# The experts of a mixture-of-experts stage: blocks of 64 rows in plain fp32 on halves of the array, in place of blocks of 128 rows in split products

## The chip, the cores and the metric

The kernel runs on one core of a Trainium2 chip. The metric is the device time of one execution in microseconds. The core has five engines with a queue each: TensorE (PE: matmuls and transposes into the eight PSUM banks), VectorE (DVE), ScalarE (ACT), GpSimd (POOL) and SyncE (SP, which here only issues DMAs). They meet through semaphores; each engine's instructions start in the order written.

## The reference

Two networks run one after the other on 512 tokens of width 1024, everything in fp32. The first has a recurrent group, a banded attention, a cross attention on a memory of 256 rows, and a mixture of 32 experts; the second has two layers with attention and a feed-forward part. Only the experts matter here:

```python
# ht: (512, 1024); every token goes to 2 of 32 experts, with weights combine_w
def expert_block(args):                  # a block of rows of one expert
    xb, e = args
    g = xb @ w_gate[e]                   # (rows, 1024) @ (1024, 512)
    u = xb @ w_up[e]                     # (rows, 1024) @ (1024, 512)
    return (jax.nn.silu(g) * u) @ w_down[e]   # (rows, 512) @ (512, 1024)
ys = lax.map(expert_block, (xs, block_expert))
contrib = ys[dest] * w_sorted[:, None]
y = zeros((512, 1024)).at[tok_sorted].add(contrib)     # then x + y, and two norms
```

With the reference's inputs the 1024 (token, expert) pairs fall on the 32 experts as 35 42 69 32 24 45 40 43 21 7 30 35 45 21 28 23 33 48 31 61 61 41 28 25 20 21 15 22 24 11 27 16. The kernel finds this on the chip; any routing has to work.

## The kernel before

**Products.** Nearly all products are split: a matrix is written as a high part in fp32r and a low part, the rest, and high x high, high x low and low x high are summed in PSUM, three matmuls for one. ScalarE writes the high parts, VectorE subtracts to get the low ones. For the experts' weights these are `weights_high` (L722, the activation at L726) and `weights_low` (L556, L558), in six units an expert: 0 and 1 gate, 2 and 3 up, 4 and 5 down.

**Ahead of the experts.** The cross attention ends with its output product (TensorE L1953), to which the router's products are added (L2085). `moe_tensor` (L448) turns the normed rows (`rows(HR, n)`, L458); ScalarE evacuates them scaled (L734) and stores each row twice to `rows_scratch` in DRAM (L736), 1 MB per tile of 128 tokens. VectorE works out the routing in some forty small operations (L564 to L640). The rank of each pair within its expert comes from triangular matmuls (L468, L472), and the list of rows of every expert from eight matmuls on one-hot ranks (L475), which leave `idx` (L611). Then TensorE turns the rows of X (L458 again), which ScalarE keeps as `AUX` (L747).

**The loop.** A block holds up to 128 rows of one expert. GpSimd gathers its rows from DRAM (`gather`, L406); TensorE turns them (`turn_x`, L484), ScalarE and VectorE split them (L754, L647). `unit` (L487, matmuls L494) takes the six units in order: 48 matmuls of 128x512 for gate and up, 24 for down. In between come silu (L767), the product with up (L662), its transposes (L522) and its split (L783, L670). The down product of a block runs behind the gate and up products of the next. Its 128x1024 result is evacuated (`lay_y`, L759, L760) and stored to `expert_rows` in DRAM at its rows' places by an indirect DMA (`store`, L409). The three weight matrices of an expert, 2 MB each, are loaded by SyncE (L358, L362) into `ring[0]`, `ring[1]` and `ring[2]`, one buffer each, as soon as both parts of the previous one are split. Blocks beyond the 32nd, for experts with more than 128 rows, use lists from a table in DRAM (`slot_tokens`, L417, L421); there are none with these inputs.

**Behind the loop.** SyncE loads the stored rows back (L389); VectorE adds both of a token's rows, weighted, to X (L699, L700) and multiplies by the norm's weights (L702); ScalarE sums rows and squares (L808, L810, L811); two roots (L814, L815) and a scaling (L715, L818) follow; TensorE turns the result back (L545), and the first layer's products begin (L1031).

The next lines are the heart of the loop on TensorE.

```python
for k in range(n_k):
    for q, (i, w) in enumerate(((0, e_high(u)), (0, e_low(u)), (1, e_high(u)))):
        for j in range(n_j):
            mm = pe.matmul(acc[j][:, :], xs[i][:, (u % 2) * n_k + k, :], w[:, n_j * k + j, :], ...)
```

The attention further behind has plain fp32 matmuls on parts of the array: `pe_pairs` (L1717) has two heads in the two halves of the rows for the scores (L1729) and in the two halves of the columns for the values (L1744), each followed by transposes (L1760). L1068 is a plain fp32 sum over partitions with the whole array.

Of the kernel before, what the change touches and what calls it, by code (L numbers as in the profile page):

```python
# [37 lines left out]
SLOTS = 2 * T  # L38
OVER = (SLOTS - 1) // (P + 1)
MAXB = EXPERTS + OVER  # L40
MINB = EXPERTS
ABSENT = 2 * SLOTS
# [36 lines left out]
CONSTS = [("ident", P), ("ones", P), ("lower", P), ("pair", P), ("perm", P), ("perm32", P), ("desc", EPG), ("count", P), ("slot", 2 * TT)]  # L79
# [34 lines left out]
def build(nc, A, out):  # L114
    with ExitStack() as ctx:
# [71 lines left out]
        s_bias = sem("bias_ready")  # L187
# [57 lines left out]
        slots = sb("slots", [P, 2, TT], U32)  # L245
        ids = sb("ids", [P, 2, TT], U32)
        absent = sb("absent", [P, OVER], U32)
# [4 lines left out]
        LAG = 3  # L252
        idx_more = sb("idx_more", [P, 2 + LAG], U32)
        rows_dram = nc.dram_tensor("rows_scratch", (SLOTS, D), F32).ap()
        slot_dram = nc.dram_tensor("slot_tokens", ((LAG + 1 + OVER + 2 * TT) * P, 1), U32).ap()
        y_dram = nc.dram_tensor("expert_rows", (SLOTS, D), F32).ap()
        HT = S[:, 0:8, :].rearrange("p (t a) n -> p t (a n)", t=TT)
        XROW = AUX[:, :, :].rearrange("p (t a) n -> p t (a n)", t=TT)
        FROW = X[:, 0:2, :].rearrange("p a n -> p (a n)")
        Y = [[S[:, 4 * t + 2 * w:4 * t + 2 * w + 2, :].rearrange("p a n -> p (a n)") for w in range(2)] for t in range(TT)]  # L260
        JUNK = [S[:, 16:18, :].rearrange("p a n -> p (a n)"), S[:, 18:20, :].rearrange("p a n -> p (a n)"), QKVG[:, 0:2, :].rearrange("p a n -> p (a n)")]
        HR = MKV[:, 0:DC, :]
# [20 lines left out]
        hot_ids = S[:, 20, 0:2 * TT * EXPERTS].rearrange("p (w t n) -> p w t n", w=2, t=TT)  # L283
# [4 lines left out]
        XB = S[:, 8:10, :].rearrange("p a n -> p (a n)")  # L288
        XBT = [SP[:, i:i + 2, :].rearrange("p a (c s) -> p (a c) s", s=P) for i in (10, 12)]
        SG, PR = S[:, 16, :], S[:, 17, :]  # L290
        AT = [SP[:, i, :].rearrange("p (c s) -> p c s", s=P) for i in (14, 15)]


        EW = [XH, XL, SP]

        def e_raw(u, b=None):
            if isinstance(b, str):
                return QKVG[:, 4 * u - 8:4 * u - 4, :]
            if isinstance(b, int) and b == 1 and u < 4:
                return QKVG[:, (8, 0)[u // 2] + 4 * (u % 2):(8, 0)[u // 2] + 4 * (u % 2) + 4, :]  # L300
            return ring[u // 2][:, 4 * (u % 2):4 * (u % 2) + 4, :]

        def e_high(u):
            return EW[u % 3][:, 0:4, :]

        def e_low(u):
            return EW[u % 3][:, 4:8, :]

        def as_f32(a):
            return a.bitcast(F32)  # L310

        YB = S[:, 18:20, :]
# [5 lines left out]
        scattered = sem("slot_tokens_stored")  # L318
        counted_waits = sem("counted_waits")
        last_landed = sem("last_down_landed")  # L320
        idx_landed, xb_landed = sem("idx_landed"), sem("rows_gathered")
        g_landed, u_landed, d_landed = sem("gate_w_landed"), sem("up_w_landed"), sem("down_w_landed")

        ew_high, ew_low, ew_used = sem("expert_w_high"), sem("expert_w_low"), sem("expert_w_used")
        x_turned, x_high, x_low = sem("x_turned"), sem("expert_x_high"), sem("expert_x_low")
        sg_done, pr_done = sem("silu_done"), sem("product_done")
        a_turned, a_high, a_low, y_a, y_stored = (sem(n) for n in ("a_turned", "a_high", "a_low", "y_laid", "y_stored"))
        y_sum, y_stat, y_root, y_out, y_back = sem("y_weighted"), sem("y_sums"), sem("y_root"), sem("y_scaled"), sem("y_turned_back")

        def expert_w(w, e):  # L330
            return w[bass.ds(e, 1)].rearrange("o p n -> p (o n)")
# [6 lines left out]
        def expert_w(w, e):  # L338
            return w[bass.ds(e, 1)].rearrange("o p n -> p (o n)")

        def wait_counted(eng, sem_, value):

            eng.wait_ge(sem_, value)
            eng.sem_inc(counted_waits, 1)

        def moe_sync(sp):
            sp.wait_ge(wl_done, UA)
            sp.dma_start(flat(ring[0]), expert_w(A["expert_gate_w"], 0)).then_inc(g_landed, 16)
            sp.wait_ge(cross_low, DC)
            sp.dma_start(QKVG[:, 0:8, :].rearrange("p a n -> p (a n)"), expert_w(A["expert_up_w"], 1)).then_inc(u_landed, 16)  # L350
            sp.wait_ge(res_done, 16)
            sp.dma_start(flat(ring[1]), expert_w(A["expert_up_w"], 0)).then_inc(u_landed, 16)
            sp.dma_start(flat(ring[2]), expert_w(A["expert_down_w"], 0)).then_inc(d_landed, 16)

            def gate_up(b, e):
                for i, (w, landed) in enumerate((("expert_gate_w", g_landed), ("expert_up_w", u_landed))):
                    wait_counted(sp, ew_low, 2 + 2 * i if isinstance(b, int) else b * 6 - 4 + 2 * i)
                    sp.dma_start(flat(ring[i]), expert_w(A[w], e)).then_inc(landed, 16)  # L358

            def down(b, e):  # L360
                wait_counted(sp, ew_low, b * 6 + 6)
                sp.dma_start(flat(ring[2]), expert_w(A["expert_down_w"], e)).then_inc(d_landed, 16)  # L362

            gate_up(2, 2)
            sp.wait_ge(rows_turned, 2 * TT)
            sp.dma_start(FROW, A["final_row"].to_broadcast([P, D])).then_inc(s_const, 16)
            down(1, 1)
            with sp.Fori(3, EXPERTS - 1) as b:
                gate_up(b, b)
                down(b - 1, b - 1)  # L370
            sp.wait_ge(slots_done, 1)
            nb = sp.value_load(table_u[0:1, 63:64], min_val=MINB, max_val=MAXB)
            with sp.Fori(EXPERTS - 1, nb) as b:
                e = sp.value_load(table_u[0:1, bass.ds(b - (EXPERTS - 2), 1)], min_val=0, max_val=EXPERTS - 1)
                gate_up(b, e)
                e0 = sp.value_load(table_u[0:1, bass.ds(b - (EXPERTS - 1), 1)], min_val=0, max_val=EXPERTS - 1)
                down(b - 1, e0)
            final = sp.value_load(table_u[0:1, 62:63], min_val=MINB - 1, max_val=MAXB - 1)
            e = sp.value_load(table_u[0:1, bass.ds(final - (EXPERTS - 2), 1)], min_val=0, max_val=EXPERTS - 1)
            sp.dma_start(LAST_DOWN, expert_w(A["expert_down_w"], e)).then_inc(last_landed, 16)  # L380

        LAST_DOWN = QKVG[:, 8:16, :].rearrange("p a n -> p (a n)")

        def load_y(sp):
            nb = sp.value_load(table_u[0:1, 63:64], min_val=MINB, max_val=MAXB)
            wait_counted(sp, y_stored, nb * 16)
            for t in range(TT):
                for w in range(2):
                    sp.dma_start(Y[t][w], y_dram[w * T + t * P:w * T + (t + 1) * P, :]).then_inc(s_x[t], 16)  # L389

# [2187 lines left out]
```

## Time and profile before

| | us |
|---|---|
| median of 3 runs | 2368.01 |
| lowest and highest | 2367.68, 2375.88 |
| span of the profiled execution | 2372.1 |
| of it from the first expert product (470.89) to the last (1070.94) | 600.1 |
| from there to the first product of the layers (1109.33) | 38.4 |

Times of instructions come from the one profiled execution. The granted clock is TensorE's, as a share of 2.4 GHz; 0.50 is the lower of its two levels, 1.2 GHz. A matmul's record lasts longer than it keeps the array, so in a row of them the distance of their starts counts, which is the whole time less the last record, divided by their number less one. A plain fp32 matmul leaves two records, a split one one for each of its three. A shape such as 128*64 128x128 reads: stationary operand of 128 rows and 64 columns, 128 moving columns. "idle before" is the time in which the engine stood still ahead of the instruction, with what ended it.

### The profile page before, as it was taken

How to read it: one execution, taken by the hardware profiler on the slowest of the kernel's cores; microseconds unless marked ns; L12 is line 12 of the kernel's file. 1: busy time of each engine (PE TensorE's matmuls, PEld its weight loads, DVE VectorE, ACT ScalarE, POOL GpSimd, SP SyncE). 2: the span in 40 equal slices, each digit the busy share in tenths (PEclk: the TensorE clock that was granted, in tenths of full speed). 3: DMA queues.
4: the chain of work that ended last, by engine and by line, in shares of the span. 5: the costliest groups of instructions: out<-in, count | busy, mean ns of one | idle time of the engine just before them, and what ended most of it. 6: DMA issues, size and time to landing. Idle time of an engine off the chain costs nothing.

```text
span 2372.1 us, 27297 instructions
## 1 busy us (share of the span) xinstructions
PE 2177.1 (92%) x10430; PEld 1735.9 (73%) x10430; DVE 1574.2 (66%) x1872; ACT 1190.0 (50%) x1444; POOL 204.9 (9%) x155
## 2 busy tenths in 40 slices
PE   6998999799999999994978899999989798999997
PEld 4786778677877777773745688888766466888875
DVE  6557624378888888885777576465567857656565
ACT  4645533367777777775457332222245645222223
POOL 1000000121111111110010012011100100111020
PEclk9999999799999999997999999999999999999998
DMA  5241130569999999974210122222321002322221
GB/s 197 99 174 55 72 124 18 236 208 363 356 356 354 357 360 359 352 298 146 105 36 1 54 90 105 89 90 106 108 84 58 36 19 72 107 89 94 102 93 50
DMA packets 48814, 359.98 MB, mean 152 GB/s; under 512 B 12224, under 2 KB 13416, under 8 KB 21456
## 3 DMA queue, kind: packets, MB, share of 16 engines
q1 hardware_dynamic: 36880, 340.89, 39.0%
q0 software_dynamic: 10752, 13.60, 1.8%
q10 hardware_dynamic: 1088, 4.19, 0.4%
q8 instruction: 64, 1.05, 0.2%
q14 instruction: 30, 0.25, 0.0%
HBM read 360.71 MB, written 25.72 MB: 163 GB/s over the span
## 4 chain that ended last, share of the span: by engine, by line
PE 76%; DVE 10%; ACT 9%; issue 3%; DMA 2%; ACTq 0%; SPq 0%; DVEq 0%; POOLq 0%
PE bank L1031 41%; PE bank L494 15%; PE bank L1953 10%; DVE split_products L558 3%; ACT split_products L726 2%; PE bank L484 1%; PE bank L1744 1%; ACT S L1810 1%; PE bank L1978 1%; PE bank L1729 1%; PE bank L2041 1%; DVE X L1282 1%; ACT S L1821 1%; DVE split_weights L1237 1%; PE bank L1760 1%
## 5 line engine op out<-in xcount | busy, mean ns | idle before, releaser
L1031 PE MATMUL bank<-split_x_high,split_weights 128*128 128x512 f32 x2144 | 670.5, 393 | 31.1 <-DVE split_x_low L1251 14.7
L1245 ACT ACTIVATE split_weights<-ring 128x2048 fp32r<-128x2048 f32 (+1 forms) x122 | 228.2, 1872 | 561.6 <-PE bank L1031 522.8
L1031 PEld LDWEIGHTS bank<-split_x_high,split_weights 128*128 128x128 f32 x2144 | 406.1, 189 | 121.6 <-issue 36.8
L1237 DVE TENSOR_TENSOR split_weights<-ring,split_weights 128x2048 fp32r<-128x2048 f32 (+1 forms) x122 | 276.5, 2267 | 186.8 <-ACT split_weights L1245 186.7
L1031 PE MATMUL bank<-split_products,split_weights 128*128 128x512 f32 x1200 | 333.0, 394 | 4.5 <-DVE split_products L1437 4.5
L1031 PE MATMUL bank<-split_x_low,split_weights 128*128 128x512 f32 x800 | 312.6, 391 | 0.0
L1031 PEld LDWEIGHTS bank<-split_products,split_weights 128*128 128x128 f32 x1200 | 228.3, 191 | 54.0 <-DVE split_products L1437 6.0
L494 PE MATMUL bank<-split_products 128*128 128x512 f32 x768 | 189.5, 395 | 11.8 <-DVE split_products L558 11.8
L494 PE MATMUL bank<-split_x_high,split_products 128*128 128x512 f32 x768 | 192.2, 400 | 6.8 <-DVE split_x_high L558 4.7
L494 PE MATMUL bank<-split_x_low,split_products 128*128 128x512 f32 x768 | 189.5, 396 | 1.9 <-DVE split_products L670 1.9
L558 DVE TENSOR_TENSOR split_products<-ring,split_products 128x2048 fp32r<-128x2048 f32 x62 | 142.1, 2292 | 64.1 <-ACT split_products L726 61.5
L494 PEld LDWEIGHTS bank<-split_products 128*128 128x128 f32 x768 | 141.8, 188 | 53.6 <-DVE split_products L558 24.5
L1031 PEld LDWEIGHTS bank<-split_x_low,split_weights 128*128 128x128 f32 x800 | 151.0, 189 | 31.2
L494 PEld LDWEIGHTS bank<-split_x_high,split_products 128*128 128x128 f32 x768 | 144.5, 192 | 36.7 <-DVE split_x_high L558 5.0
L1953 PE MATMUL bank<-split_x_high,split_weights 128*128 128x512 f32 x512 | 162.5, 396 | 7.2 <-DVE split_x_low L2130 7.2
L1009 POOL TENSOR_TENSOR QKVG<-QKVG 128x512 f32<-128x512 f32 x44 | 97.8, 2223 | 810.5 <-DVE QKVG L1451 723.9
L494 PEld LDWEIGHTS bank<-split_x_low,split_products 128*128 128x128 f32 x768 | 143.5, 190 | 30.7 <-DVE split_x_low L558 2.2
L558 DVE TENSOR_TENSOR split_x_high<-ring,split_x_high 128x2048 fp32r<-128x2048 f32 x62 | 141.9, 2288 | 24.8 <-ACT split_x_high L726 17.1
L558 DVE TENSOR_TENSOR split_x_low<-ring,split_x_low 128x2048 fp32r<-128x2048 f32 x62 | 141.9, 2288 | 1.7 <-ACT split_x_low L726 1.7
L726 ACT ACTIVATE split_products<-ring 128x2048 fp32r<-128x2048 f32 x62 | 119.3, 1924 | 43.7 <-PE bank L494 30.7
L726 ACT ACTIVATE split_x_high<-ring 128x2048 fp32r<-128x2048 f32 x62 | 119.0, 1920 | 6.5 <-PE bank L494 6.5
L726 ACT ACTIVATE split_x_low<-ring 128x2048 fp32r<-128x2048 f32 x62 | 118.7, 1915 | 0.9 <-DMA ring<-in_expert_down_w 0.4
(426 smaller groups left out, 2945.4 us busy)
## 6 DMA issues: line engine op xcount, KB each, us to landing
ring<-in_expert_gate_w SPq DMA_DIRECT2D x31, 2048.0 KB, 8.1
ring<-in_expert_up_w SPq DMA_DIRECT2D x31, 2048.0 KB, 7.6
ring<-in_expert_down_w SPq DMA_DIRECT2D x31, 2048.0 KB
ring<-in_ffn_w_up SPq DMA_DIRECT2D x44, 1024.0 KB, 4.8
ring<-in_w_in SPq DMA_DIRECT2D x26, 1024.0 KB, 4.8
ring<-in_ffn_w_down SPq DMA_DIRECT2D x16, 1024.0 KB, 4.7
ring<-in_w_out SPq DMA_DIRECT2D x12, 1024.0 KB, 4.8
ring<-in_ffn_w_down SPq DMA_DIRECT2D x8, 768.0 KB, 4.1
```

Source lines behind the costliest of these rows:

```text
L484: mm = pe.transpose(bank[4 + j][:, c * P:(c + 1) * P], XB[:, (4 * j + c) * P:(4 * j + c + 1) * P], ident)
L494: mm = pe.matmul(acc[j][:, :], xs[i][:, (u % 2) * n_k + k, :], w[:, n_j * k + j, :], start=(u % 2 == 0 and k == 0 and q == 0), stop=(u % 2 ...
L558: dve.tensor_tensor(e_low(u), e_raw(u, b), as_f32(e_high(u)), ALU.subtract).then_inc(ew_low, 1)
L726: act.activation(e_high(u), e_raw(u, b), ACT.Copy).then_inc(ew_high, 1)
L1009: st.tell(pool.tensor_tensor(QKVG[:, 14 + i, :], QKVG[:, b, :], QKVG[:, 4 + b, :], ALU.mult), f_act)
L1031: mm = pe.matmul(acc[:, :], w[:, u, k, m], x, start=first and q == 0, stop=last and q == 2)
L1237: st.tell(dve.tensor_tensor(w[:, 1, 0:ks, 0:nc_], raw_half(g)[:, :, 0:nc_], as_f32(w[:, 0, 0:ks, 0:nc_]), ALU.subtract), wl_done)
L1245: st.tell(act.activation(WHL[g % 2][:, 0, 0:ks, 0:nc_], raw_half(g)[:, :, 0:nc_], ACT.Copy), wh_done)
L1282: st.do(dve.scalar_tensor_tensor(X[:, c, :], bank[a][:, :], -1.0 / D, X[:, c, :], ALU.mult, ALU.add))
L1729: pe.matmul(bank[2 * (p % cfg["depth"]) + i][:, 0:x["keys"]], q, k, start=True, stop=True).then_inc(s["scored"], 1)
L1744: mm = pe.matmul(bank[7 - x["j"] % 2][r, t], v(kt), PT[:, i, kt, t], start=(kt == 0), stop=(kt == last))
L1953: mm = pe.matmul(accs[i][:, 0:n], w[:, u, k, i * P:(i + 1) * P], x, start=(k == order[0] and q == 0), stop=(k == order[-1] and q == 2))
```

## The change

- **Blocks of 64 rows** instead of 128. Blocks for more than 64 rows of an expert run behind the 32 in a loop of their own, at least once.
- **No split.** Weights and rows stay plain fp32. Gate and up of a block share bank 6: up in the lower 64 partitions, gate in the upper 64, a matmul of 128x64 each per chunk of 128. Down has its two halves of 512 columns in the two halves of bank 2.
- **Nine weight buffers** (`EWG`, `EWU`, `EWD`, three each) instead of three, placed over tensors that are free by then; the loads of expert 0 and of 1's gate are issued during the cross attention, that of unit 29 of its output weights behind them.
- **Rows are added on chip.** The 64 result rows of a block are spread to the 512 tokens by eight matmuls with a one-hot matrix that holds the combine weights (`CW`, built by VectorE from a count and the list of tokens), 64 rows each, alternating between the two halves of the rows and over the banks 0, 1, 3 and 7; VectorE adds each from PSUM to `XROW`, the kept rows of X. The stores to `expert_rows`, their read-back and the table in DRAM are gone; the rows are stored once to `rows_scratch`. Three further listings by `AT_RANK` give the weights and the lists of the further blocks.
- **Behind the loop** VectorE multiplies and sums rows in one operation; ScalarE takes the two sums of squares.
- In the layers some pairs of semaphores are merged into one with doubled counts; nothing else changes there.

```diff
+        EWG = (QKVG[:, 8:16, :], MKV[:, :, :], ring[2][:, :, :])
+        EWU = (AUX[:, :, :], ring[0][:, :, :], H[:, :, :])
+        EWD = (QKVG[:, 0:8, :], ring[1][:, :, :], X[:, :, :])
+        SETS = 3
+        COMB = (0, 1, 3, 7)
@@ moe_sync
+            for b in range(SETS, EXPERTS):
+                s = b % SETS
+                sp.wait_ge(gu_used[s], b // SETS)
+                load_expert(sp, EWG[s], "expert_gate_w", b, gu_landed[s])
+                load_expert(sp, EWU[s], "expert_up_w", b, gu_landed[s])
+                sp.wait_ge(dn_used[s], b // SETS)
+                load_expert(sp, EWD[s], "expert_down_w", b, d_landed[s])
@@ moe_gpsimd
+            for b in range(EXPERTS):
+                if b >= 2:
+                    pool.wait_ge(x_turned, b - 1)
+                gather(b % 2, idx[0:SLOT, b:b + 1])
@@ moe_tensor
+            def gate_up(i, s):
+                for k in range(DC):
+                    pe.matmul(bank[6][0:SLOT, :], XBT[i][:, k, :], EWU[s][:, k, :], start=(k == 0), stop=(k == DC - 1))
+                    mm = pe.matmul(bank[6][SLOT:P, :], XBT[i][:, k, :], EWG[s][:, k, :], start=(k == 0), stop=(k == DC - 1))
+                mm.then_inc(gu_used[s], 1)
+            def down(i, s):
+                for k in range(HC):
+                    for h in range(2):
+                        mm = pe.matmul(bank[2][SLOT * h:SLOT * h + SLOT, :], AT[i][:, k, :], EWD[s][:, 2 * k + h, :], start=(k == 0), stop=(k == HC - 1))
+                mm.then_inc(dn_used[s], 1)
+            def spread(i, q):
+                t, h = divmod(q, 2)
+                r = slice(SLOT * h, SLOT * h + SLOT)
+                pe.matmul(bank[COMB[q % 4]][:, :], CW[i][r, t * P:(t + 1) * P], YS[i][r, :], start=True, stop=True).then_inc(comb_done, 1)
+            def combine(b):
+                pe.wait_ge(ys_laid, b + 1)
+                pe.wait_ge(c_built, max(b + 1, 2))
+                for q in range(8):
+                    if 8 * b + q >= 4:
+                        pe.wait_ge(acc_done, 8 * b + q - 3)
+                    spread(b % 2, q)
+            for b in range(EXPERTS):
+                s = b % SETS
+                pe.wait_ge(gu_landed[s], 32 * (b // SETS + 1))
+                pe.wait_ge(x_laid, b + 1)
+                if b:
+                    pe.wait_ge(pr_done, b)
+                gate_up(b % 2, s)
...
+                if b >= 2:
+                    combine(b - 2)
+                if b + 1 < EXPERTS:
+                    pe.wait_ge(xb_landed[(b + 1) % 2], 16 * ((b + 1) // 2 + 1))
+                    turn_x((b + 1) % 2)
+                if b:
+                    expert_down(b - 1)
+                pe.wait_ge(pr_done, b + 1)
+                turn_product()
+            combine(EXPERTS - 2)
+            expert_down(EXPERTS - 1)
+            combine(EXPERTS - 1)
@@ moe_vector
+            for b in range(EXPERTS):
+                dve.wait_ge(sg_done, b + 1)
+                product()
...
+                if b >= 2:
+                    added(b - 2)
+                build_main(b)
@@ moe_scalar
+            for b in range(EXPERTS):
+                act.wait_ge(gu_used[b % SETS], b // SETS + 1)
+                if b:
+                    act.wait_ge(a_turned, b)
+                gate()
+                if b + 1 < EXPERTS:
+                    act.wait_ge(x_turned, b + 2)
+                    lay_x((b + 1) % 2)
+                if b:
+                    expert_y(b - 1)
+                act.wait_ge(a_turned, b + 1)
+                if b >= 2:
+                    act.wait_ge(dn_used[(b - 2) % SETS], (b - 2) // SETS + 1)
+                lay_product(b % 2)
```

The extra loop has the same steps in series with buffer 0 alone: `turn_x(0)`, `gate_up(0, 0)`, `turn_product()`, `down(0, 0)`, then eight of `spread(0, q)`.

## Rows read from the trace of the kernel before

**Rows 1.** The page, part 1: busy us (share of the span) and instructions.

```profile
PE 2177.1 (92%) x10430; PEld 1735.9 (73%) x10430; DVE 1574.2 (66%) x1872; ACT 1190.0 (50%) x1444; POOL 204.9 (9%) x155
```

**Rows 2.** Busy times by stretch: from:to, length, each engine, granted clock, DMA share, GB/s.

```profile
516.15:1063.50 547.35, 533.97 (x2488) 434.64 (x2488) 471.39 (x296) 419.56 (x356) 61.78 (x62) 1.00 0.93 353
```

**Rows 3.** Chain of waits in the expert loop: start us, us, what.

```profile
516.15 5.75 PE bank L494 x24
...
534.55 5.74 PE bank L494 x24
```

**Rows 4.** Timeline inside one block: start us, us, engine, line, operation, out<-in, shape.

```profile
534.19 0.60 ACT L767 ACTIVATE S<-bank 128x512 f32<-128x512 f32 x1 [0.22 <-PE bank L494]
...
540.13 1.03 PE L484 MATMUL bank<-konst,S 128*128 128x128 f32 x8
...
548.63 0.69 DVE L670 TENSOR_TENSOR split_products<-bank,split_products 128x512 fp32r<-128x512 f32 x1
```

**Rows 5.** Groups of instructions in 516.15 to 1063.5: busy us, mean ns, idle before.

```profile
L558 DVE TENSOR_TENSOR split_products<-ring,split_products 128x2048 fp32r<-128x2048 f32 x59 | 135.2, 2292 | 56.1 <-ACT split_products L726 53.4 <-issue 2.5
```

**Rows 6.** Timeline of plain fp32 matmuls in the layers behind, on TensorE.

```profile
1177.71 1.88 PE L1068 MATMUL bank<-S,konst 128*128 128x512 f32 x4
...
1276.45 1.13 PE L1729 MATMUL bank<-QKVG 64*128 64x512 f32 x4
1277.78 1.09 PE L1744 MATMUL bank<-S 128*64 128x128 f32 x16 [0.20 <-ACT S L1821]
1278.80 0.98 PE L1760 MATMUL bank<-konst,S 128*128 128x128 f32 x7
```

**Rows 7.** DMA by stretch: from:to, length, granted clock, DMA share, GB/s.

```profile
419.00:421.00 2.00, 1.00 1.04 442
...
598.40:599.40 1.00, 1.00 1.01 311
...
600.40:603.40 3.00, 1.00 1.01 430
```

**Rows 8.** DMA view of 516.15 to 1063.5.

```profile
DMA packets 21417, 193.24 MB, mean 353 GB/s; under 512 B 8125, under 2 KB 8125, under 8 KB 9952
```

**Rows 9.** Ahead of the first block: chain of waits, then timeline.

```profile
444.36 15.52 DMA rows_scratch<-S
...
470.89 13.96 PE bank L494 x48
...
446.40 3.62 PE L475 MATMUL bank<-S,gatew 128*128 128x32 f32 x16 [1.55 <-DVE gatew L607]
```

**Rows 10.** TensorE by stretch: from:to, length, busy and records, granted clock, DMA share, GB/s.

```profile
1255.00:1265.00 10.00, 6.07 (x46) 0.85 0.00 0
1275.00:1285.00 10.00, 9.61 (x92) 1.00 0.01 2
450.00:460.00 10.00, 3.32 (x17) 0.67 0.75 312
```

**Rows 11.** Chain of waits behind the last block.

```profile
1063.58 7.36 PE bank L494 x24
...
1072.90 2.57 DMA expert_rows<-S,idx_more
...
1075.93 4.49 DMA S<-expert_rows
```

**Rows 12.** Timeline behind the last block.

```profile
1083.16 1.06 ACT L808 ACTIVATE S<-S 128x1024 f32<-128x1024 f32 x1 [7.52 <-DVE S L700]
1083.16 1.23 DVE L702 TENSOR_TENSOR S<-S,X 128x1024 f32<-128x1024 f32 x1
1084.13 0.19 ACT L808 ACTIVATION_READ_ACCUMULATOR S<-S 128x1 f32 x1
...
1097.95 1.28 ACT L814 ACT_TABLE_LOAD   x1
...
1109.33 0.48 PE L1031 MATMUL bank<-split_x_high,split_weights 128*128 128x512 f32 x1
```

More of the change, by code:

```diff
@@ L472, in moe_tensor, with listed @@
                 mm = pe.matmul(bank[7][:, 64:64 + EXPERTS], ones, M[:, t, :], start=(t == 0), stop=(t == TT - 1))
+            def listed(out_, hot):
+                for n in range(2 * TT):
+                    mm = pe.matmul(out_, AT_RANK[:, n, :], hot(n), start=(n == 0), stop=(n == 2 * TT - 1))
+                return mm
             pe.wait_ge(mask_done, 2)
-            for n in range(2 * TT):
-                mm = pe.matmul(bank[7][:, 0:EXPERTS], AT_RANK[:, n, :], hot_ids[:, n // TT, n % TT, :], start=(n == 0), stop=(n == 2 * TT - 1))
@@ L618, in moe_vector @@
+            over, end, begin = (rt(EXPERTS) for i in range(3))
+            step(dve.tensor_scalar(count_u[:, :], bank[7][:, 64:64 + EXPERTS], -1.0, 0.0, ALU.add, ALU.max))
+            step(dve.tensor_scalar(count_u[:, :], count_u[:, :], 6, None, ALU.logical_shift_right))
+            step(dve.tensor_copy(over, count_u[:, :]))
             step(dve.tensor_tensor_scan(end, ones[:, 0:EXPERTS], over, 0.0, ALU.mult, ALU.add))
             step(dve.tensor_tensor(begin, end, over, ALU.subtract))
-            step(dve.tensor_tensor(flat_rank, flat_hots, begin[:, None, :].to_broadcast([P, 2 * TT, EXPERTS]), ALU.mult))
@@ new lines, in product, with build, add_rows, added @@
+            def product():
+                return dve.tensor_tensor(SG, SG, bank[6][0:SLOT, :], ALU.mult).then_inc(pr_done, 1)
+            def build(i, tok, w):
+                return dve.tensor_scalar(CW[i], IOTA, tok, w, ALU.is_equal, ALU.mult).then_inc(c_built, 1)
+            def add_rows(q):
+                t, h = divmod(q, 2)
+                x = XROW[:, t, h * 512:(h + 1) * 512]
+                return dve.tensor_tensor(x, x, bank[COMB[q % 4]][:, :], ALU.add).then_inc(acc_done, 1)
+            def added(b):
+                if b:
+                    dve.wait_ge(acc_done, 8 * b)
+                for q in range(8):
+                    dve.wait_ge(comb_done, 8 * b + q + 1)
+                    add_rows(q)
@@ L1182, in layernorm @@
                     pe.wait_ge(r_free, last_add)
[L1183 removed]
+                    pe.matmul(acc[:, :], ones, X[:, DC - 1, :], start=False, stop=True).then_inc(ln_stat, 1)
                     acc = bank[b]
```

581 lines of the change are left out of this document (237 added, 344 removed).

## The prediction

> **What bounds the kernel now.** I read the page first, then the busy times by stretch, then the chain of waits, then the trace inside the stage that the change rewrites. The page says that TensorE is busy 92% of the span, VectorE 66 and ScalarE 50 [rows 1]. That is an average over stages; the change touches only some 435 to 1110 us, and in the loop there TensorE is busy 534.0 of 547.4 us, DMA 0.93 of the time at 353 GB/s, VectorE 471.4, ScalarE 419.6 [rows 2]. So the expert loop has one engine at its limit and the transfers right under it. The chain starts one expert at 516.15 and the next at 534.55, so an expert costs 18.4 us [rows 3]. Of these 72 products of a split block take 24 per 5.75 us, thus 17.3 us [rows 3], and the transposes most of the rest, eight in 1.03 us and four more [rows 4]; short waits on VectorE's split close the gap (VectorE itself waits mostly for ScalarE's half [rows 5]). What ends last in this stage is TensorE's own work, three matmuls for each product of the reference. Whoever replaces these wins only down to what the transfers allow.
>
> **What one plain fp32 product costs.** Each plain matmul leaves two records. Two matmuls on the whole array with 512 columns show four records in 1.88 us, the last lasting 0.59: starts are (1.88 - 0.59) / 3 = 0.43 us apart, so one matmul takes 0.86 us, against 3 x 0.24 = 0.72 us for the three split ones [rows 3, 6]. Alone it would be slower. The gain must come from halves of the array. The attention's value products put two heads in the two column halves: 16 records (eight matmuls 128x64, 128 columns) in 1.09 us, last one 0.27: 0.82 / 15 = 0.055 us per record, where a whole-array record of 128 columns cannot be under 0.43 / 4 = 0.107. So pairs run side by side. Row halves do too: four records of 512 columns, two score matmuls, in 1.13 us, not 1.88 [rows 6]. A change of shape costs about 0.1 us: the last value record starts at 1277.78 + 1.09 - 0.27 = 1278.60, runs 0.11, and the transposes begin at 1278.80 [rows 6]; four changes a block are 0.4 us. The Trainium skill (TensorEngine Tiling (Array Packing), Key Properties) speaks against the change here: a change of the tiling mode drains the engine. If each drain showed a record's whole tail of about 0.16 us (0.59 - 0.43), a block would take 0.2 us more; the trace shows the smaller price.
>
> **One block after the change.** T is the end of the gate and up products.
> - Gate and up: 8 chunks, one pair each, 8 x 0.86 = 6.9 us; down: 4 x 0.86 = 3.4 us.
> - Spreading rows into tokens: 8 matmuls in four pairs, 3.4 us if nothing holds them. But they use four banks, and the fifth waits for the first of eight VectorE additions. These queue behind the product of gate and up, which waits for the silu: 0.2 + 0.6 (ScalarE, 128x512) + 0.03 + 0.69 (VectorE) = 1.5 us after T [rows 4]. An addition is a 128x512 tensor_tensor from PSUM, 0.69 us [rows 4]; four of them bring the eighth matmul to T + 4.3, and it ends at T + 5.2. Behind this new wait stand, on TensorE's queue, the next rows' transposes, the down products and the next gate and up, so it is paid in full.
> - Twelve transposes of 64 rows: between a half and all of the 0.13 us each of now [rows 4]; I take 1.2 us, nearer to the whole, because they remain separate instructions.
> - Sum: 6.9 + 5.2 + 3.4 + 1.2 + 0.4 = 17.1 us; if the transposes of the next rows run beside the last spreading matmul, 16.2. I take 16.7.
> - VectorE: 0.7 + 8 x 0.69 + one 128x512 build of the one-hot (bounds 0.3 to 0.7) = about 6.8 us; ScalarE: four evacuations, 2.2 us. Both disappear as limits; VectorE matters by its place, above.
> - Transfers: 6.29 MB of weights an expert, plus gathered rows (about 32 x 4 KB). Within a transfer 442 and 430 GB/s are moved, and around a new load's start 311 for about a us [rows 7]; three loads at 430 are 14.6 us, and 0.5 lost for each gives 16.1 us. The stage's mean at full share would be 353 / 0.93 = 380 GB/s, 16.6 us [rows 2, 8]. The ends are thus 14.6 and 16.6, the second the nearer row. With three sets of buffers the loads queue up, so TensorE's 16.7 stays just the larger. Stores of results and their read-back vanish (small beside 193 MB [rows 8]).
>
> **How many blocks.** Now 32 experts fill 32 blocks. From the reference with its inputs I counted the tokens: the largest expert has 69, the next two 61. Above 64 needs a second block: one extra, which the new code runs at least once anyway. 33 blocks.
>
> **Start.** The chain now waits 15.5 us from 444.36 for the stored rows and starts the first products at 470.89 [rows 9]. The change stores 2 MB, not 4, and takes the first split out of ScalarE's queue; the index list is ready when TensorE's 3.6 us of ranking end at 450.0 [rows 9], the rows are then stored already, the transposes of X (7.4 us, at the lower clock, 0.67 in this stretch [rows 10]) are next, and the first gate product starts at 459. It pays about 3 us for the lower clock, as the first block does now. T of block 0 is 469. Then come silu with its table load, the second listing and transposes, 3.4 us, so T of block 1 is 479.3; two more listings (3.8 us at full clock, half of the 3.6 for each), down and transposes, 8.8 us: T of block 2 is 495.0. The three further listings lie in blocks 0 and 1, where no spreading is due. GpSimd loses its stores and scatters; gathers go out two blocks ahead. On SyncE, the loads of expert 0 and 1 are moved ahead of the last unit of the cross attention's output weights: it waits for the score and value counts, but that unit is split only at about 407, over 20 us after those counts; hidden.
>
> **Main run.** 29 x 16.7 = 484.3: T of block 31 is 979.3.
>
> **End.** Behind it, in order: spreading of 29 (5.2), down of 30 and transposes (4.0), evacuation and spreading of 30 (0.4 + 4.8), down of 31 (3.5), evacuation (0.8), first spread and eight additions (1.0 + 5.5): 25.2 us. The extra block's transposes can start at T + 23.4, when the last spreading matmul ends; its weights were asked for after block 30's gate and have landed. Then nothing hides its chain: transposes and evacuation 1.8, gate and up 6.9, silu and product 1.6, turn 1.1, down 3.5, evacuation 0.8, additions 6.5, with 1 for register loads. Its end comes 46.5 us after T, 1025.8.
> Now 38.4 us lie between the last down product (1063.58 + 7.36) and the layer's first product at 1109.3; the store and read-back of rows are 2.6 and 4.5 of these [rows 11]. After the change: four row sums on VectorE, of which the first, 1.3 us, is exposed; per tile two ScalarE sums of 1.06 + 0.19 us [rows 12], 10 us; then the same 11.4 us of roots, scaling and transposes up to the layer. 1025.8 + 1.3 + 10 + 11.4 + 0.4 = 1048.9. The two weight splits for the layer lie beside these sums; their loads stand on SyncE behind those of the extra block and are asked for some 40 us ahead of need. The layers behind are unchanged, their merged counters wait for the same matmuls.
>
> **Sum.** 1109.3 - 1048.9 = 60.4 us less. The profiled execution spans 2372.1 us, 4 more than the median of 2368.0; the difference goes on the median: 2307.6, say 2308.
>
> **Rivals.**
> - Transfers stay the limit at the present mean: speaks for it that DMA is at 0.93 already [rows 2], and a new load's start slows those in flight [rows 7]. 6.42 MB at 353 GB/s are 18.2 us, 1.5 more for about 30 blocks: 2353. The Trainium skill (DMA: Bandwidth & Descriptors, Specifications) gives about 358 GB/s as a core's limit from HBM; an estimate from it is 17.9 us an expert and 2345 in all. The trace's 442 GB/s over 2 us disagrees [rows 7]. Chance 0.13.
> - Shorter blocks, 15.9 us, with transposes beside spreading and loads at 430: 29 x 0.8 less: 2285. Chance 0.10.
> - Slower: the halves don't overlap while 512-column streams of two different weights are read beside loads. Its place is gate, up, down and spreading: 10.3 + 1.7 us more a block, 33 times: 396 us, 2704. It decides once a block exceeds 16.7 + 60 / 31 = 18.7 us, that is, if less than four fifths of the overlap holds. Against it: pairs start together both in row and column halves [rows 6], but no transfer ran there. Chance 0.05.
> - The granted clock falls. Stretches with TensorE busy 6.1 of 10 us have 0.85, with 9.6 they have 1.00 [rows 10]; the new block has gaps in spreading, busy some 0.85. At 0.85 throughout, 12.3 us of array work become 14.5: 65 us, 2373; at the lower level all along it would be near 2680. Chance 0.07.
> - It doesn't do what it says: another routing with four or more extra blocks of some 20 us each in series takes the gain. The counts say one. Chance 0.02; other costs that I don't see, 0.03.
>
> **How the numbers follow.** My forecast has 0.60: its own range 2292 to 2325 (block 16.2 to 17.2). With the shorter blocks and most of the transfer rival in, 2282 to 2345 holds 8 in 10. A measurement tells apart about 0.5%, 12 us. Faster: 0.60 + 0.10 + 0.13 and a part of the clock case, 0.86; same 0.04; slower 0.10.
>
> **What would show it.** Starts of two following blocks' gate products 16.7 us apart; pairs of records starting together; the eighth spreading matmul waiting for VectorE; weight loads landing before their matmuls; first gate product near 459; the layer's first product near 1049. TensorE idle before gate products with a DMA named as releaser would mean the transfer rival; records one behind the other, 0.43 us apart, the serial one; a granted clock under 1.00 in the loop, the clock one.

## The result, and the profile after

The changed kernel takes 2292.21 us (median of four runs, 2288.16 to 2296.66) beside 2369.7 for the kernel before on the same chip: a ratio of 0.9657, 95% interval 0.964 to 0.9675. The forecast was 2308 us, in a range of 2282 to 2345, so direction and range hold, and the kernel is some 16 us faster than forecast. The profiled executions span 2294.8 and 2372.1 us: 77.3 us less, where the steps gave 60.4.

Busy time and instructions of the whole span after the change, part 1 of the page, beside [rows 1]:

```profile
PE 2133.1 (93%) x10298; PEld 1471.7 (64%) x10298; DVE 1254.3 (55%) x1889; ACT 799.3 (35%) x1184; POOL 156.8 (7%) x106
```

Busy times by stretch (from:to, length, each engine, granted clock, DMA share, GB/s), the expert loop and what follows it; the first answers to [rows 2]:

```profile
498.00:959.00 461.00, 458.43 (x2204) 172.92 (x2204) 171.69 (x290) 59.84 (x116) 26.43 (x28) 1.00 0.99 400
...
959.00:1030.00 71.00, 46.26 (x195) 20.70 (x192) 35.89 (x60) 25.23 (x38) 0.00 (x0) 0.86 0.32 120
```

TensorE is busy for 458.4 of 461.0 us at full clock. VectorE fell from 471.4 of 547.4 us to 171.7 of 461, ScalarE from 419.6 to 59.8. The DMA share is 0.99 at 400 GB/s. So two things are at their limit here at once, and the page alone can't say which of them sets the block.

The chain of waits, three blocks (start us, us, what), which answers to [rows 3]:

```profile
534.64 3.65 PE bank L443 x16
...
550.55 3.65 PE bank L443 x16
...
566.47 3.65 PE bank L443 x16
```

L443 is the down projection; its starts are 15.91 us apart, and stay so to 0.01 us from block 3 to block 31. The forecast had 16.7. Inside one block (timeline: start us, us, engine, line, operation, out<-in, shape, count; in brackets idle time before, and its releaser):

```profile
554.53 0.64 PE L429 MATMUL bank<-AUX,S 128*64 128x512 f32 x1
...
561.02 0.59 PE L429 MATMUL bank<-AUX,S 128*64 128x512 f32 x1
561.02 0.59 PE L430 MATMUL bank<-QKVG,S 128*64 128x512 f32 x1
...
561.55 4.56 PE L450 MATMUL bank<-S 64*128 64x512 f32 x15
561.66 0.59 ACT L744 ACTIVATE S<-bank 64x512 f32<-64x512 f32 x1 [6.54 <-PE bank L430]
...
562.29 0.68 DVE L639 TENSOR_TENSOR S<-S,bank 64x512 f32<-64x512 f32 x1 [9.99 <-ACT S L744]
...
562.89 4.86 DVE L647 TENSOR_TENSOR S<-S,bank 128x512 f32<-128x512 f32 x8
563.62 0.29 PEld L450 LDWEIGHTS bank<-S 64*128 64x128 f32 x2 [0.92 <-DVE S L647]
564.22 0.29 PEld L450 LDWEIGHTS bank<-S 64*128 64x128 f32 x2 [0.30 <-DVE S L647]
...
565.95 0.59 PE L450 MATMUL bank<-S 64*128 64x512 f32 x1
565.96 0.47 PE L423 MATMUL bank<-konst,S 64*128 64x64 f32 x5
...
566.47 3.65 PE L443 MATMUL bank<-X,rstd 128*64 128x512 f32 x16
...
570.05 0.46 PE L436 MATMUL bank<-konst,S 64*128 64x64 f32 x4
...
570.44 0.64 PE L429 MATMUL bank<-ring,S 128*64 128x512 f32 x1
```

The records of up (L429) and gate (L430) start together: the column halves run side by side. The spreading (L450) gets its first four products out at once; then each weight load waits for an addition of VectorE (L647), every 0.60 us. The list of waits for 500 to 959 us has this as the only wait of TensorE for another engine's work (who waits, for whom: us in total, times, longest), four times in each of 29 blocks, and none for a load:

```profile
PEld bank L450 <- DVE S L647: 53.0, 116, 0.9
```

The transposes of the next rows (L423) lie beside the last spreading record. Four parts cover the block: gate and up 554.53 to 561.55, 7.02 us; spreading and transposes to 566.47, 4.92; down to 570.05, 3.58; product transposes to 570.44, 0.39. Their sum is 15.91.

The chain behind the last block:

```profile
959.50 0.60 ACT S L744
...
978.07 4.89 PE bank L450 x16
983.25 0.70 PE bank L423 x8
...
995.67 5.37 PE bank L443 x16
...
1008.76 1.23 DVE S L702
...
1030.32 4.80 PE bank L1018 x21
```

The extra block runs alone, from its transposes at 983.25 to the first row sum (L702) at 1008.76. Its down projection takes 5.37 us where a main block's takes 3.65. The granted clock is 0.86 over the whole stretch behind the loop, and 0.70 over this projection:

```profile
995.60:1001.30 5.70, 5.35 (x16) 1.77 (x16) 0.00 (x0) 0.00 (x0) 0.00 (x0) 0.70 0.00 0
```

The layer's first product comes at 1030.32, before the change at 1109.33 [rows 12].

### The profile page after: what moved, and what is told of

Read it like the earlier page. It is cut to its first block, busy times and chain, and to the rows that moved or that the text cites. A ratio compares the mean times of both kernels' runs of the same rounds, so it can differ in the third digit from the quotient of the medians.

```text
span 2294.8 us, 25318 instructions
## 1 busy us (share of the span) xinstructions
PE 2133.1 (93%) x10298; PEld 1471.7 (64%) x10298; DVE 1254.3 (55%) x1889; ACT 799.3 (35%) x1184; POOL 156.8 (7%) x106
## 3 DMA queue, kind: packets, MB, share of 16 engines
q8 instruction: 82, 1.34, 0.2%
## 4 chain that ended last, share of the span: by engine, by line
PE 82%; DVE 8%; ACT 6%; issue 3%; DMA 1%; SPq 0%; DVEq 0%; ACTq 0%; POOLq 0%
PE bank L1018 42%; PE bank L1947 10%; PE bank L429 10%; PE bank L443 5%; PE bank L450 4%; PE bank L1738 1%; ACT S L1804 1%; PE bank L1972 1%; DVE S L647 1%; PE bank L1723 1%; PE bank L2035 1%; DVE X L1269 1%; ACT S L744 1%; ACT S L1815 1%; DVE split_weights L1224 1%
## 5 line engine op out<-in xcount | busy, mean ns | idle before, releaser
L1018 PEld LDWEIGHTS bank<-split_x_high,split_weights 128*128 128x128 f32 x2144 | 407.1, 190 | 122.2 <-issue 36.8
L647 DVE TENSOR_TENSOR S<-S,bank 128x512 f32<-128x512 f32 x264 | 160.4, 673 | 17.4 <-PE bank L450 17.2
L450 PE MATMUL bank<-S 64*128 64x512 f32 x528 | 161.8, 628 | 5.3 <-ACT S L750 2.4
L450 PEld LDWEIGHTS bank<-S 64*128 64x128 f32 x528 | 62.2, 185 | 104.1 <-DVE S L647 58.5
L1947 PEld LDWEIGHTS bank<-split_x_high,split_weights 128*128 128x128 f32 x512 | 97.4, 190 | 30.0 <-issue 9.7
L429 PE MATMUL bank<-AUX,S 128*64 128x512 f32 x192 | 86.6, 605 | 2.0 <-ACT S L741 2.0
L430 PE MATMUL bank<-QKVG,S 128*64 128x512 f32 x192 | 86.7, 605 | 0.0
L1804 ACT ACTIVATE S<-S,stats 128x512 f32<-128x512 f32 (+3 forms) x96 | 63.7, 664 | 50.5 <-DVE stats L1777 25.4
L429 PE MATMUL bank<-ring,S 128*64 128x512 f32 x176 | 77.9, 595 | 0.5 <-issue 0.5
L430 PE MATMUL bank<-MKV,S 128*64 128x512 f32 x176 | 77.9, 595 | 0.0
L1436 DVE TENSOR_SCALAR QKVG<-bank,cols 128x512 f32<-128x512 f32 x44 | 35.6, 810 | 73.5 <-PE bank L1018 73.5
```

The source lines that it names most:

```text
L429: pe.matmul(bank[6][0:SLOT, :], XBT[i][:, k, :], EWU[s][:, k, :], start=(k == 0), stop=(k == DC - 1))
L430: mm = pe.matmul(bank[6][SLOT:P, :], XBT[i][:, k, :], EWG[s][:, k, :], start=(k == 0), stop=(k == DC - 1))
L450: pe.matmul(bank[COMB[q % 4]][:, :], CW[i][r, t * P:(t + 1) * P], YS[i][r, :], start=True, stop=True).then_inc(comb_done, 1)
L647: return dve.tensor_tensor(x, x, bank[COMB[q % 4]][:, :], ALU.add).then_inc(acc_done, 1)
L1018: mm = pe.matmul(acc[:, :], w[:, u, k, m], x, start=first and q == 0, stop=last and q == 2)
L1804: st.tell(act.activation(SS[:, u % 4, 0:n], SS[:, u % 4, 0:n], ACT.Exp, bias=stats[:, 0, u:u + 1], scale=1.0 if pairs[p]["bias"] else -1.0 ...
```

## Experiments

The question was which of the two full resources sets 15.91 us, and whether the steps of the forecast are the right ones. Theory: TensorE sets it, with its spreading held up by VectorE's additions. Rivals: the transfers set it; the halves gain nothing; the move of the loads costs something ahead of the experts.

**The halves one after the other** (e1_order):

```
 for k in range(DC):
     pe.matmul(bank[6][0:SLOT, :], XBT[i][:, k, :], EWU[s][:, k, :], ...)
+for k in range(DC):
     mm = pe.matmul(bank[6][SLOT:P, :], XBT[i][:, k, :], EWG[s][:, k, :], ...)
```

> The same matmuls in the same halves of the array, but gate_up issues all eight up matmuls first and then all eight gate matmuls; nothing else is changed and the result is that of the reference. Theory (the two column halves run side by side only because neighbours in the queue use different halves): gate and up take 16 x 0.86 = 13.7 us instead of 7.0, a block 22.6 instead of 15.9, and 33 blocks cost 33 x 6.7 = 221 us: about 2513 us. Rival (the gain comes from the missing split and the smaller stationary operand, not from the halves; 64 columns would be cheap in any order): a block stays at 15.9 and the time at 2292.

Measured: 2462.95 us, blocks of 21.10 us, so 5.19 more. TensorE's timeline of this kernel (L429 is up, L431 gate):

```profile
560.17 5.79 PE L429 MATMUL bank<-H,S 128*64 128x512 f32 x13
565.38 0.64 PE L431 MATMUL bank<-ring,S 128*64 128x512 f32 x1
565.80 0.59 PE L429 MATMUL bank<-H,S 128*64 128x512 f32 x1
565.86 0.59 PE L431 MATMUL bank<-ring,S 128*64 128x512 f32 x1
```

The side-by-side run is real and carries the change: without it in gate and up alone, the kernel is slower than before (2376.36 us beside it on the same chip). The size was off (2513 us and 22.6 a block were expected), and the lines say why: the first gate record starts at 565.38, beside up's thirteenth, though all gate products stand behind all up products in the program. Four gate records run beside the last four of up, so 28 records' places are used in place of 32. (So the statement ahead of the prediction that an engine's instructions start in the order written does not hold for these records.) Side by side they take 16; 12 more at 0.43 are 5.2 us.

**Additions ahead of the product on VectorE** (e2_adds_first):

```
 for b in range(EXPERTS):
+    if b >= 2:
+        added(b - 2)
     dve.wait_ge(sg_done, b + 1)
     product()
 ...
-    if b >= 2:
-        added(b - 2)
     build_main(b)
```

> VectorE adds the eight spread pieces of block b-2 before it multiplies silu and up of block b, instead of after; same result. Theory (TensorE sets the block, and in it the eighth spreading matmul waits for the fourth addition, which waits behind silu and product): additions start 0.9 us after gate and up instead of 1.4 to 1.5, the fourth ends at about 3.3 instead of 4.2, so the eighth matmul starts about 0.8 us earlier and a block takes 15.1 us; over 30 blocks 24 us less, about 2268. Rival (transfers set the block: DMA share 0.99 at 400 GB/s in the loop): a block stays at 15.9 and the time within 5 us of 2292, with TensorE waiting for weights instead.

Measured: ratio 0.9627 (0.9604 to 0.9651), blocks of 15.81 us: 0.10 less where 0.8 was expected. The timeline of this kernel:

```profile
560.47 4.46 PE L450 MATMUL bank<-S 64*128 64x512 f32 x15
...
561.70 4.87 DVE L647 TENSOR_TENSOR S<-S,bank 128x512 f32<-128x512 f32 x8 [9.89 <-PE bank L450]
562.44 0.29 PEld L450 LDWEIGHTS bank<-S 64*128 64x128 f32 x2 [0.81 <-DVE S L647]
```

The additions start 1.23 us behind the first spreading record, instead of 1.34 (562.89 less 561.55). What was in front of them, silu and product, had cost only 0.1 us, because the first spread product is not there much earlier. From then on the pitch of 0.60 us rules as before. So VectorE's order is not the lever; the wait of the fifth to eighth product for an addition still is.

**No spreading** (e3_no_spread): the spreading products and the additions of the 32 main blocks are left out, their counts are raised by bare increments.

> Leaves out the spreading matmuls and the additions of the 32 main blocks (their counters are raised without work), so that the experts' rows are not added except those of the extra block. TensorE's work in a block is then 7.0 + 0.6 + 3.6 + 0.5 = 11.7 us, less than the loads can take, so the period shows the transfers' own limit. Theory: 14.6 us (430 GB/s) to 15.5, with TensorE waiting for weights; the time is about 29 x 0.4 to 1.3 plus 10 at the end less, 2245 to 2270. Rival (transfers set the block already): 15.9 us again. A third reading, that a load costs what the mean share gave in the kernel before (380 GB/s), would make it 16.6 us, which the 15.9 of now already contradicts.

Measured: 2257.51 us. The first blocks take 11.6 us, then they alternate between short ones of 11.7 to 13.8 and long ones of 17.2 to 21.3; 29 blocks take 445.3 us, the last 26 of them 15.76 on average. A stretch of the loop, and a product of up on TensorE:

```profile
600.00:900.00 300.00, 243.07 (x1148) 83.87 (x1146) 22.56 (x38) 39.20 (x76) 17.97 (x19) 0.90 1.01 410
```

```profile
629.00 1.11 PE L429 MATMUL bank<-AUX,S 128*64 128x512 f32 x1 [4.75 <-DMA AUX<-in_expert_up_w]
```

Here the transfers do bind, and the trace shows it by what was absent above: TensorE idle in front of up products with a load as releaser. Their own pace is 15.76 us a block at 410 GB/s, a little over the 14.6 to 15.5 expected. That is only 0.15 under the changed kernel's 15.91.

**A third less to load** (e8_fewer_loads), and **down between the halves of the spreading** (e5_down_between), alone and with a third less to load (e7_between_fewer_loads). In e7 and e8 the down weights of experts 3 to 31 are not loaded:

```
-    load_expert(sp, EWD[s], "expert_down_w", b, d_landed[s])
+    sp.sem_inc(d_landed[s], 16)
```

and in e5 and e7 TensorE's order is changed:

```
 if b >= 2:
-    combine(b - 2)
+    combine(b - 2, range(4))
 ...  turn_x((b + 1) % 2)
 if b:
     expert_down(b - 1)
+if b >= 2:
+    combine(b - 2, range(4, 8))
```

> The changed kernel's order, and the down weights of experts 3 to 31 aren't loaded (those of experts 0 to 2 are used again; the output isn't the reference's). Theory (the waits for additions, not the transfers, set the block): 15.91 us as before, within 0.03, about 2292 us. Rival (DMA sets the block, or contention of the loads with the engines stretches it): the block falls to 15.1 to 15.6, 2269 to 2283 us.

> TensorE's order inside a block is changed: four spreading products, the transposes of the next rows, the down projection of the block before, then the other four spreading products. In the changed kernel products 4 to 7 wait for additions 0 to 3 (one every 0.60 us), and the spreading takes 4.92 us up to the down projection where eight products at 0.43 us and the transposes beside them would take about 4.1. Theory (TensorE, held by VectorE's additions, sets the block at 15.91 us, the transfers are just behind it): the waits for additions vanish, TensorE's own block is about 15.1 us, and the blocks run at that until the stock of loaded weights is used up, then at the transfers' pace, which the kernel without spreading showed as 445.3 us for 29 blocks (15.36 on average, 15.8 in the later ones): -13 to -16 us, 2276 to 2280 us, with waits for weights and uneven blocks. Rival A (the transfers already set 15.91): blocks unchanged, 2292 us. Rival B (nothing but TensorE binds): 29 blocks at 15.1, -23 us, 2269 us.

> The reordered kernel, and the down weights of experts 3 to 31 aren't loaded (those of experts 0 to 2 are used again; the output isn't the reference's), so a third less is moved in the blocks. Theory: with the transfers out of the way TensorE's own block shows, 15.1 us (15.0 to 15.3), even to 0.02 us, no waits for weights: about 2269 us. Rival (TensorE's own block is not shorter in this order, because the reordering adds changes of shape and waits of its own): 15.4 or more, 2278 us or more.

Measured, e8: 2292.9 us, every block still 15.91. The loop of this kernel in 550 to 950 us:

```profile
550.00:950.00 400.00, 397.79 (x1914) 150.03 (x1912) 149.88 (x254) 52.19 (x101) 23.67 (x25) 1.00 0.68 266
```

The DMA share is down to 0.68 and 266 GB/s and nothing moves. The 0.99 of the changed kernel is a pace that it can just keep, not one that it waits for.

Measured, e5: ratio 0.9603 (0.9584 to 0.9622), 2279.1 us. Its chain of waits, and VectorE's timeline in the same block:

```profile
558.46 1.92 PE bank L450 x8
560.37 0.49 PE bank L423 x8
560.86 3.58 PE bank L443 x16
564.45 1.92 PE bank L450 x8
...
573.62 1.92 PE bank L450 x8
```

```profile
559.74 2.46 DVE L650 TENSOR_TENSOR S<-S,bank 128x512 f32<-128x512 f32 x4
565.54 2.48 DVE L650 TENSOR_TENSOR S<-S,bank 128x512 f32<-128x512 f32 x4 [3.34 <-PE bank L450]
```

Now VectorE adds while TensorE does the down projection, and no spreading product waits. A block takes 573.62 - 558.46 = 15.16 us, 0.75 less. It keeps that for fifteen blocks; then twelve blocks take 15.79 on average, the last two 15.16 again, and waits for loads appear, as in this line from a view of 740 to 950 us (engine, operand and line waited for, and releaser: us in total, times, longest):

```profile
PE bank L429 <- DMA ring<-in_expert_up_w: 2.6, 3, 1.6
```

Measured, e7: 2275.43 us, and all blocks 15.16, so TensorE's own block in this order is 15.16 and the 15.79 in e5 are the transfers', as in e3. (Its span of 2273.6 is the changed kernel's 2294.8 less 29 x 0.75, within 0.6; the 2269 had been reckoned from the median and from 15.1.) The three runs together settle it: waits for additions set 15.91, TensorE alone would need 15.16, the transfers 15.8. The busy share does not show such a wait: TensorE is busy for 397.8 of 400 us in e8, with the waits, and for 400.0 in e7, without them, because records of 0.59 us cover the distance of the products. e5 is also the best version found: its interval does not meet the changed kernel's 0.964 to 0.9675.

**No extra block** (e6_no_extra): the loops over further blocks are left out on all engines, so the rows beyond 64 of one expert are missing.

> The loops over further blocks are left out on all engines (their rows are missing from the output). Theory (the extra block runs serially behind the last spreading and nothing covers it): the last addition of block 31 ends about 6 us after its spreading began at 978.07, so the stretch from there to the layer at 1030.1 shortens by what lies between: extra transposes at 983.25 to its last addition at about 1006, -22 to -24 us, 2269 us; blocks stay at 15.91. Rival (the stretch behind the experts is set by the final row's or the split weights' work, which the extra block hides): under -10 us, 2282 or more.

Measured: 2270.82 us, ratio 0.9572 (0.9555 to 0.9589). The chain behind its last block (L695 is the silu, L653 the first row sum):

```profile
958.77 0.60 ACT S L695
...
982.76 0.69 DVE S L614
983.47 1.23 DVE S L653
```

From the last main silu to the first row sum are 24.7 us; in the changed kernel, from 959.50 to 1008.76, they are 49.3. So the extra block costs 24.6 us for five rows, and nothing hides it; 22 to 24 us were expected. That is more than the 29 x 0.75 = 21.8 us between the main blocks of the changed kernel and of e7.

**The early load moved back** (e4_load_later), and **the same kernel twice more** (e9_same_again, e10_same_again):

```
-if g == 26:
-    load_expert(sp, EWU[0], "expert_up_w", 0, gu_landed[0])
 if g == 28:
     sp.wait_ge(att["scored"], 48)
+    load_expert(sp, EWU[0], "expert_up_w", 0, gu_landed[0])
```

> The load of expert 0's up matrix is issued with that of its down matrix, after the cross attention's scores, instead of between two weight units of that stage; same result. In the profile the cross attention ended at 388.1 us, 5.1 later than in the kernel before, most of it in stretches with a granted clock of 0.67 and 0.83. Theory (those low stretches fall there by chance from one execution to the next): no difference in the medians, under 3 us, and low stretches elsewhere or at the same place in some. Rival (the load delays a weight unit by some us there and makes TensorE wait, and the clock falls for that): about 5 us less, 2287.

> The changed kernel, nothing edited: a second profiled execution, for the stretch ahead of the experts. In the first one the granted clock was 0.67 in 352 to 362 us and 0.83 in 382 to 392, and the first gate product began at 463.51; in two experiments whose code is the same up to there it was 1.00 in both stretches and the first gate product began at 457.57 and 456.87. Theory (where the clock is lowered ahead of the experts differs from execution to execution of the same code): the first gate product falls anywhere between 456.5 and 464, along with the clock in these two stretches. Rival (the code of the changed kernel itself sets it): 463.5 within 0.3, with 0.67 and 0.83 again. Blocks 15.91 us by both.

> The same once more. Theory: the first gate product between 456.5 and 464, not necessarily where the execution before has it, at or below 458 if the clock is 1.00 in 352 to 362 and 382 to 392. Rival: 463.5 within 0.3 both times. Blocks 15.91 us by both.

Measured: e4 has 2296.0 us, a ratio of 0.9663 (0.9638 to 0.9688), no difference from the changed kernel; the rival's 5 us less did not come. For the other two the start of the experts tells more than the time, 2288.44 and 2290.94. The stretches ahead of it and the first record of gate and up on the timeline (L429, up; gate starts beside it), of the changed kernel's first profile:

```profile
352.00:362.00 10.00, 9.60 (x46) 8.66 (x47) 3.45 (x14) 4.34 (x14) 0.00 (x0) 0.67 0.14 57
382.00:392.00 10.00, 9.76 (x54) 9.07 (x55) 1.98 (x5) 2.48 (x7) 0.00 (x0) 0.83 0.71 275
```

```profile
463.51 0.61 PE L429 MATMUL bank<-AUX,S 128*64 128x512 f32 x1 [0.78 <-ACT S L741]
```

The same of e9:

```profile
352.00:362.00 10.00, 8.90 (x64) 7.99 (x65) 4.98 (x19) 5.08 (x17) 0.00 (x0) 1.00 0.03 14
382.00:392.00 10.00, 10.00 (x49) 8.36 (x48) 1.29 (x2) 1.09 (x2) 0.00 (x0) 1.00 0.91 351
```

```profile
457.36 0.61 PE L429 MATMUL bank<-AUX,S 128*64 128x512 f32 x1 [0.78 <-ACT S L741]
```

The same of e10:

```profile
352.00:362.00 10.00, 8.77 (x48) 7.61 (x48) 4.91 (x19) 4.45 (x14) 0.00 (x0) 0.83 0.22 91
```

```profile
460.78 0.61 PE L429 MATMUL bank<-AUX,S 128*64 128x512 f32 x1 [0.78 <-ACT S L741]
```

The same code starts the experts at 463.51, 457.36 and 460.78 us, and the granted clock (0.67, 1.00, 0.83 in 352 to 362) goes with it. But these early stretches are not all of it: e7, whose code is the same up to there, has 1.00 in both and yet starts at 461.50. There the clock is low later, behind the cross attention:

```profile
435.00:445.00 10.00, 10.00 (x55) 9.58 (x55) 5.64 (x28) 5.28 (x8) 0.00 (x0) 0.59 0.45 187
```

e9 has 0.83 in this stretch. The early loads alone do not lower the clock: in e9 they run in 382 to 392 at 351 GB/s, with the clock at 1.00. The blocks are 15.91 us in e9 and e10. What decides in which execution the clock falls, and where, stays open.

## Why the forecast was right, and where it was off

The steps, by the first profile of the changed kernel; T is the end of gate and up, 0.1 us ahead of the silu.

- **What bounds the stage: right.** The work of TensorE went down until VectorE's additions held it up, and the transfers followed closely behind. All three were in the forecast in this order, and e8, e5 and e3 confirm each.
- **Price of a plain product and of the halves: right.** Records are 0.43 us apart and pairs start together. Gate and up took 7.02 with the change of shape (6.9 + 0.1), down 3.58 (3.4 + 0.1).
- **Price of a change of shape: right.** The last gate record starts at 561.02 and the first spreading record at 561.55: 0.53, 0.10 more than the pitch. The Trainium skill (TensorEngine Tiling (Array Packing), Key Properties) has the engine drained at a mode change; the weighed estimate of 0.16 for it does not show, the 0.1 of the row does.
- **The block: the failed step.** The pieces of the forecast added up to 17.1 us and it chose 16.7, between 16.2 and 17.1; measured 15.91, under both ends. Spreading was put at T + 1.5 for the first addition, 0.69 for each, the eighth product ending at T + 5.2 and transposes of 0.8 behind it, half of them hidden. Measured: first addition at T + 1.3, pitch 0.60, transposes wholly beside the last spreading record, and the down projection starting at 4.92 us behind the first spreading record. So 5.2 + 0.8 + the changes of shape, 6.2, were 4.9 (without the 0.1 counted in gate and up). The rest is the four transposes of the product, 0.39, as put. The mis-sized terms are two, and each is about 0.4 us of the 0.8 between 16.7 and 15.91: a price of one instruction (0.69 us) taken for the distance of a row of them, so that the eighth product ended at T + 4.8 and not at T + 5.2, and half of the transposes counted on the path. In the changed kernel eight additions take 4.86 us, of which the last lasts 0.67, so a start comes every 4.19 / 7 = 0.60, the same reading that gave 0.43 from 1.88 us for matmuls. It was in reach, for VectorE's timeline of the kernel before has two such instructions from PSUM in a row, whose starts are 1.28 - 0.68 = 0.60 apart:

```profile
542.36 1.28 DVE L647 TENSOR_TENSOR split_products<-bank,split_products 128x512 fp32r<-128x512 f32 x2
```

- **"Shorter blocks" was the case that came**, at 15.9 as written there, with a chance of only 0.10. Its time of 2285 was 7 too low by the median, and its reason half right: transposes beside the spreading yes, loads at 430 GB/s no, 400 to 412.
- **Transfers: right as an order, small as a number.** The forecast took 16.1 us for them, measured 15.76. Blocks of 15.91 do not refute 16.1 by themselves: the stock of loaded weights would have to bridge 29 x 0.19 = 5.5 us, and in e5 it bridged 15 x 0.6 = 9; e3 and the later blocks of e5 do. The rival with 353 GB/s falls by e3's 410 GB/s over 300 us. The Trainium skill's 358 GB/s (DMA: Bandwidth & Descriptors, Specifications), from which 2345 us followed, falls with it. The Trainium skill says elsewhere (Perfetto Trace Analysis, Roofline) that a single core may pull more than that share, up to some 435 GB/s; the trace agrees with that, at 410. It should have been read together with the first.
- **Start: right within what executions differ by, in part by luck.** 459 was forecast for the first gate product; the eleven executions show 456.9 to 463.5, 460.8 in the mean. In the profiled one the ranking ends at 455.0, forecast 450.0. From there on 9.0 us were forecast and 8.5 measured, but otherwise made up: the transposes of X took 5.6 us and not 7.4, and behind them came 1.65 us of waiting for the gathered rows, which the forecast did not have. Up to T of block 2 the start cost 2.9 us (497.9, forecast 495.0).
- **Main run:** 461.5 us for 29 blocks, forecast 484.3: 22.8 less.
- **End: right.** From T of block 31 to the layer's first product, 1030.3 - 959.4 = 70.9 us, forecast 69.6. Inside it, the extra block ended at T + 49.2 rather than 46.5, 1.9 us of it in the down projection at a clock of 0.70 (5.37 us, forecast 3.5), and what follows up to the layer took 21.7 us rather than 23.1. Without the extra block e6 shows 24.8 us up to the last addition (982.76 + 0.69 - 958.67), where the forecast's steps give 25.2.
- **Layers behind:** 1264.5 us, before 1262.8, so 1.7 more; not studied.

Together: -60.4 + 2.9 - 22.8 + 1.3 + 1.7 = -77.3 us, as measured. The main run is more than the whole error; the other three give back 5.9 us. So it is in part luck that 2292.21 still lies in the forecast's own range of 2292 to 2325, whose blocks of 16.2 to 17.2 us did not come. The other rivals got nothing: the halves ran side by side beside loads at 400 GB/s, the granted clock stayed at 1.00 in the loop, where TensorE was busy for 458.4 of 461 us, and there was one extra block. (The block time at which the serial case decides is 16.7 + 60 / 31 = 18.6, not 18.7.)

## What to carry to other kernels

Where a row of instructions paces another engine, take its pitch from the length of a whole row, not from one instruction's duration, and look at what stands behind the paced engine's wait: here the next independent work, moved into the middle of the paced row, removed the wait (0.75 us of a 15.9 us block) where a quicker start of the pacing engine brought 0.1. When two resources are both near full, take a third off one of them in an experiment: if nothing moves, it is not the one. And a gain on one of them ends at the other, so know the second limit before sizing the first: of the 0.75 us a block, the transfers at 15.8 let all of it stand only in the first fifteen blocks and in three later ones.

## What the runs showed of the hardware

- VectorE's 128x512 additions from PSUM have records of 0.67 us, yet start 0.60 us apart when they stand in a row.
- A record of a later matmul can run beside one that stands ahead of it in the program, if it goes to the other column half: four gate records ran beside up's last four (e1).
- Transfers of 2 MB held 410 GB/s over 300 us, and stock in three sets of buffers let blocks run 0.6 us quicker than that pace for fifteen blocks (e5).
- Three profiled executions of one kernel had a granted clock of 0.67, 0.83 and 1.00 in the same 10 us, and the start of the experts differed by 6.2 us.
- TensorE's busy share alone does not tell the clock: it is 0.90 in e3 with TensorE busy for 243 of 300 us, but 0.67 in one execution with 9.6 of 10 us busy and 1.00 in another with 8.9 of the same 10.
